# Loads moved up into the decay stage, and the sums split and turned inside the state chain

## The chip, the cores and the metric

The kernel runs on one core of a Trainium2 chip. The metric is the device time of one execution in microseconds.

## The reference

One inference step of a hybrid backbone, depth 1, for two requests that share weights: 128 context tokens and 2048 latent tokens, model width 1024. The layer adds a token mixer and then a mixture of 16 experts:

```python
h = rms_norm(x, norm_mix_g) * (1 + sc_a) + sh_a
u_pool, z, xbc, dt_raw = split(h @ w_in)
y_pool = multiscale_pool(u_pool, pool_w, pool_scale)
xs, bm, cm = split(silu(centred_depthwise_conv(xbc, conv_w, conv_b)))
dt_f, dt_b = softplus(dt_raw + dt_bias)              # 8 heads each way
y_f, h_f = ssd_chunked_scan(xs, dt_f, -exp(a_log_fwd), bm, cm, h0_fwd)
y_b, h_b = ssd_chunked_scan(reversed ..., h0_bwd)     # chunks of 128 tokens
y = rms_norm((y_f + y_b + d_skip * xs) * silu(z), ssm_norm_g)
x = x + g_a * (concat(y_pool, y) @ w_out)
h = rms_norm(x, norm_ffn_g) * (1 + sc_m) + sh_m
x = x + g_m * expert_choice_ffn(h, w_router, w_gate, w_up, w_down)
```

Inside a scan, with `a_cum` the cumulative sum of `dt * a` over the 128 tokens of a chunk:

```python
cb = cc @ bc^T ;  y_diag = (cb * exp(a_cum[l] - a_cum[s], l >= s)) @ X
chunk_state = bc^T @ (X * exp(a_cum[-1] - a_cum))
h_next = h * exp(a_cum[-1]) + chunk_state             # serial over chunks
y_off  = (cc @ h_enter) * exp(a_cum)
```

## The kernel before

The kernel is a row of stages: `front` (norm, input projection, convolution, pooling, adaLN), `decays`, `back_states`, `mixer`, `selection`, `experts`, `final`. Each stage opens a block in which every engine has its own list of instructions; the next stage's instructions start when all engines have come to the end of theirs. DMAs still in flight may cross that border. Tokens are handled in 17 tiles of 128, tile 0 being the context. `front` leaves its results in the DRAM tensor `mixed`: 16 slots of 128 channels by 2176 tokens, of which slots 0 to 3 are the pooled part, 4 to 7 z, 8 to 11 x, 12 and 13 B, 14 and 15 C.

`decays` makes, for all tiles at once, a table `tab` of dt, its product with the rate, the exponentials of the sums, the weight of each token towards its chunk's end (`T_WEND`) and each chunk's decay (`T_DEC`). ScalarE loads an activation table and takes two exponentials (of the rates, L984, and of -|v|, L986). VectorE works out a softplus by a polynomial (L1032 to L1045, each step waiting for the one before). GpSimd fills and cuts the masks and the selector `pick` (L966 to L978). TensorE spreads the gate rows (L1007) and sums over tokens with triangular matrices. At the end VectorE splits the sums `v` into three bf16 parts in `stack` (L1058 to L1062), TensorE turns the 17 tiles of `stack` (L1019) and ScalarE copies them to `acum_t` (L998, L999), which only `mixer` reads.

`back_states` runs the backward chain of states. SP loads the two initial states and then one chunk at a time (six slots of `mixed`, 384 KB) into two buffers `xb`. TensorE turns the states (L1135), makes the router's shift rows (L1140, 16 matmuls), and then in round n turns chunk n (`turn`, L1150 and L1152) and multiplies chunk n-1 (`states`, L1163). ScalarE copies the B part (`bt`, L1184) and rounds one eighth of W_out (L1192), whose 512 KB it asks for itself (L1173, L1188) as soon as one of two staging buffers is free. VectorE in round n weights chunk n (`weigh`, L1212), carries the state over chunk n-1 (`carry`: decay L1221, add L1226) and makes the low part of an eighth of W_out (`low_w`, L1203). GpSimd stores each state (256 KB, two buffers `hb`) to the DRAM tensor `back` (L1109), and ends when all stores have landed.

`mixer` then takes the 17 tiles in order: SP loads `mz` (z, x, B, C), `hbt` (the stored state), `mp` (pooled part) and `xs` (residual rows) for tile i into two buffers each, the first two tiles at once. TensorE first adds up the decay exponents of tile 0 (`decay_rows`, from `acum_t`), ScalarE takes their exponentials, and then tile 0 is turned (L1364) and copied (L1501).

## Time and profile before

| what | value |
|---|---|
| median of 3 runs | 2522.24 us (2519.3 to 2522.86) |
| profiled execution, its own time | 2521.52 us |
| its span in the profile | 2519.9 us |
| TensorE busy in the span | 90% |
| VectorE / ScalarE / GpSimd busy | 55% / 40% / 9% |

The span is the profiled execution from its first instruction to its last; its own time is measured around it. All stretches below are in microseconds from the span's start. A duration behind an instruction's name is that of the group in its line; the bracket is how long the engine sat idle before it, and what released it.

### The profile page before, as it was taken

The page shows a single profiled execution, that of the slowest core. Times are in us where ns is not written, and L with a number is a line of the kernel's source. Part 1 is how long each engine was busy: PE and PEld are TensorE (multiplying, and loading weights), DVE is VectorE, ACT ScalarE, POOL GpSimd, SP SyncE. Part 2 cuts the span into 40 slices and gives each one's busy share as a digit, 9 for nine tenths or more (in the row PEclk, how much of TensorE's full clock was granted, in tenths as well). Part 3 has the DMA queues.
Part 4 walks back from the last instruction along what each step waited for, and adds up shares of the span by engine and source line. Part 5 has one row for each costly group of instructions (what it writes and reads, how often), then busy time and mean ns, then how long its engine had stood idle before and what let it go on. Part 6 is the DMA issues. An engine that isn't in the chain of part 4 may idle for free. (4 is left out here: it accounts for less than half of the span.)

```text
span 2519.9 us, 40046 instructions
## 1 busy us (share of the span) xinstructions
PE 2261.8 (90%) x15772; PEld 2052.0 (81%) x15772; DVE 1381.2 (55%) x2184; ACT 998.2 (40%) x1734; POOL 238.3 (9%) x307
## 2 busy tenths in 40 slices
PE   4999999956799999629999999999999999999980
PEld 2878887855688887518999999999999999999980
DVE  2655443226477777464566456655565555645543
ACT  3642222222455554104444444444444344434424
POOL 0000000021111111000100111101010110011010
PEclk8999999987799999758999999999999999999995
DMA  8533442216344443033665565656565655556537
GB/s 277 180 114 120 144 144 96 88 60 223 91 138 138 139 139 117 34 118 103 192 195 167 176 193 177 200 160 187 176 209 154 183 181 188 173 176 188 176 94 285
DMA packets 318699, 396.57 MB, mean 157 GB/s; under 512 B 12014, under 2 KB 273150, under 8 KB 316558
## 3 DMA queue, kind: packets, MB, share of 16 engines
q1 hardware_dynamic: 287406, 287.67, 35.7%
q0 software_dynamic: 22400, 86.06, 11.7%
q10 hardware_dynamic: 8800, 21.56, 2.3%
q8 instruction: 62, 1.02, 0.2%
q14 instruction: 31, 0.25, 0.0%
HBM read 318.12 MB, written 77.14 MB: 157 GB/s over the span
## 5 line engine op out<-in xcount | busy, mean ns | idle before, releaser
L2227 DVE TENSOR_TENSOR experts_wlo<-experts_raw,experts_whi 128x2048 fp32r<-128x2048 f32 x192 | 439.9, 2291 | 421.8 <-ACT experts_whi L2171 421.8
L2109 PE MATMUL experts_ps_r<-experts_xhi,experts_whi 128*128 128x272 f32 x2048 | 605.2, 296 | 5.4 <-DVE experts_xlo L2281 5.4
L2109 PE MATMUL experts_ps_r<-experts_xhi,experts_wlo 128*128 128x272 f32 x2048 | 593.8, 290 | 0.0
L2109 PE MATMUL experts_ps_r<-experts_xlo,experts_whi 128*128 128x272 f32 x2048 | 590.5, 288 | 0.0
L2109 PEld LDWEIGHTS experts_ps_r<-experts_xhi,experts_whi 128*128 128x128 f32 x2048 | 386.1, 189 | 8.5 <-DVE experts_xlo L2281 5.5
L2109 PEld LDWEIGHTS experts_ps_r<-experts_xlo,experts_whi 128*128 128x128 f32 x2048 | 386.9, 189 | 0.0
L2109 PEld LDWEIGHTS experts_ps_r<-experts_xhi,experts_wlo 128*128 128x128 f32 x2048 | 386.1, 189 | 0.0
L2171 ACT ACTIVATE experts_whi<-experts_raw 128x2048 fp32r<-128x2048 f32 x192 | 366.1, 1907 | 14.6 <-DMA experts_raw<-in_w_gate 13.8
L2109 PE MATMUL experts_ps_r<-experts_hhi,experts_whi 128*128 128x272 f32 x1024 | 299.6, 293 | 0.2 <-DVE experts_hlo L2301 0.2
L2109 PE MATMUL experts_ps_r<-experts_hhi,experts_wlo 128*128 128x272 f32 x1024 | 296.3, 289 | 0.0
L2109 PE MATMUL experts_ps_r<-experts_hlo,experts_whi 128*128 128x272 f32 x1024 | 294.8, 288 | 0.0
L521 PE MATMUL front_ps<-front_hhi,front_whi 128*128 128x384 f32 (+1 forms) x640 | 236.1, 369 | 0.0
L521 PE MATMUL front_ps<-front_hhi,front_wlo 128*128 128x384 f32 (+1 forms) x640 | 230.8, 361 | 0.0
L521 PE MATMUL front_ps<-front_hlo,front_whi 128*128 128x384 f32 (+1 forms) x640 | 230.8, 361 | 0.0
L2195 ACT ACTIVATE experts_hhi<-experts_hid 128x272 fp32r<-128x272 f32 x128 | 55.2, 431 | 353.9 <-DVE experts_hid L2298 353.9
L2109 PEld LDWEIGHTS experts_ps_r<-experts_hhi,experts_whi 128*128 128x128 f32 x1024 | 192.7, 188 | 1.1 <-DVE experts_hlo L2301 0.5
L2109 PEld LDWEIGHTS experts_ps_r<-experts_hlo,experts_whi 128*128 128x128 f32 x1024 | 193.0, 188 | 0.0
L2109 PEld LDWEIGHTS experts_ps_r<-experts_hhi,experts_wlo 128*128 128x128 f32 x1024 | 192.6, 188 | 0.0
L521 PEld LDWEIGHTS front_ps<-front_hhi,front_whi 128*128 128x128 f32 x640 | 120.8, 189 | 25.4 <-ACT front_u L659 12.6
L659 ACT ACTIVATE front_u<-front_ps 128x128 f32<-128x128 f32 (+2 forms) x90 | 40.2, 469 | 248.9 <-PE front_ps L521 227.9
L2049 POOL DMA_INDIRECT x<-experts_yo,experts_idx x48 | 72.1, 1502 | 684.1 <-DVE experts_yo L2288 521.1
L2190 ACT ACTIVATE experts_sg<-experts_ps_r 128x272 f32<-128x272 f32 x128 | 51.0, 398 | 214.9 <-PE experts_ps_r L2109 214.9
(393 smaller groups left out, 3453.5 us busy)
## 6 DMA issues: line engine op xcount, KB each, us to landing
experts_raw<-in_w_gate SPq DMA_DIRECT2D x64, 1024.0 KB, 5.0
experts_raw<-in_w_up SPq DMA_DIRECT2D x64, 1024.0 KB, 5.0
experts_raw<-in_w_down SPq DMA_DIRECT2D x64, 1024.0 KB, 5.3
shared_whalf<-in_w_ada SPq DMA_DIRECT2D x16, 1024.0 KB, 5.2
mixer_mz<-mixed SPq DMA_DIRECT2D x17, 768.0 KB, 7.9
mixed<-front_acc POOLq DMA_DIRECT2D x9, 1024.0 KB, 4.2
resid<-early_xin POOLq DMA_DIRECT2D x17, 512.0 KB, 3.7
mixer_xs<-resid SPq DMA_DIRECT2D x17, 512.0 KB, 4.0
```

Of the source, the lines that this page charges most:

```text
L521: mm = pe.matmul(ps[:, out, 0:n], wt[buf][:, kk, :], h[:, kk, t0:t0 + n], start=(kk == 0 and q == 0), stop=(kk == KD - 1 and q == 2))
L659: ins = act.activation(dst_u[:, uo:uo + pn], ps[:, bank_of(s), po:po + pn], func)
L2049: pool.indirect_dma_start(io["x2"], bass.IndirectOffsetOnAxis(idx[2][0:n, a:a + 1], 0), yo[0:n, a, :], None, compute_op=ALU.add).then_inc( ...
L2109: mm = pe.matmul(dst, w[:, c % RING, kk, cols], r[:, kk, :], start=(kk == 0 and q == 0), stop=(kk == KD - 1 and q == 2))
L2171: act.activation(whi[:, c % RING, :, :], raw[:, c % RAW, :, :], ACT.Copy).then_inc(whi_done, 1)
L2190: act.activation(sg[:, ft % 2, :], ps_r[:, (2 * ft) % 4, 0:ROWS], ACT.Silu).then_inc(silu_done, 1)
L2195: act.activation(hhi[:, ft, :], hid[:, ft % 2, :], ACT.Copy).then_inc(hhi_done, 1)
L2227: dve.tensor_tensor(wlo[:, c % RING, :, :], raw[:, c % RAW, :, :], whi[:, c % RING, :, :].bitcast(F32), ALU.subtract).then_inc(wlo_done, 1)
```

## The change

In `decays`, SP now issues the loads of both states and of the first four chunks, and ScalarE issues all eight loads of W_out before its first exponential. GpSimd clears `wrs` and the zero half of `hf` there, behind the masks. The split of the sums, their turning and copying leave `decays`: VectorE does the five steps of the split in `back_states` between the decay and the add of `carry`, in rounds 1, 2 and 3 (`between`); TensorE turns four tiles of sums at a time in rounds 4 to 8 (`turn_sums`) into one PSUM bank, and ScalarE copies them in its rounds 5 to 9. The low parts of W_out come in rounds 4 to 11 and the router's weights in round 12. The shift rows are made in round 2, behind the first two products. The chunk buffer is four deep, the state buffer three deep, W_out is staged whole. The loops over rounds, which ran partly in registers, are written out. At its end SP loads the first two tiles of `mixer`, whose SP begins with the one state of tile 1.

```diff
-        v, mag, e, z, z2, poly, relu = (k.sb(f"sp_{n}", [P, NT, HH]) for n in ("v", "mag", "e", "z", "z2", "poly", "relu"))
+        v = g.v_acum
+        mag, e, z, z2, poly, relu = (k.sb(f"sp_{n}", [P, NT, HH]) for n in ("mag", "e", "z", "z2", "poly", "relu"))
         aexp = k.sb("aexp", [P, HH])
-        rest = k.sb("rest", [P, NT, HH])
-        stack = k.sb("stack", [P, NT, N3], BF16)
...
+
+        @block.sync
+        def _(sp):
+            for d, name in enumerate(("state_ssm_fwd", "state_ssm_bwd")):
+                sp.dma_start(g.st[:, d, :, :], io[name][0, 0].rearrange("(a h) d n -> (h d) a n", a=4)).then_inc(g.st_loaded, 16)
+            for n in range(NB_X):
+                load_back(sp, g, io, n)
...
+            pool.memset(g.wrs[:, :, :, :], 0.0)
+            pool.memset(g.hf[:, 0, :], 0.0)
...
             act.preload_act_table_set("natural_log_exp_and_others")
-            act.activation(aexp[:, :], g.rows[:, R_ALOG:R_ALOG + HH], ACT.Exp).then_inc(aexp_done, 1)
+            w_out = io["w_out"][0].rearrange("(k p) n -> p k n", p=P)
+            for kk in range(KD):
+                act.dma_start(g.stg[:, kk, :], w_out[:, kk, :]).then_inc(g.wo_loaded[kk // 4], 16)
+            act.activation(aexp[:, :], g.rows[:, R_ALOG:R_ALOG + HH], ACT.Exp).then_inc(scalar_done, 1)
             act.wait_ge(mag_done, 1)
-            act.activation(e[:, :, :], mag[:, :, :], ACT.Exp, scale=-1.0).then_inc(exp_done, 1)
+            act.activation(e[:, :, :], mag[:, :, :], ACT.Exp, scale=-1.0).then_inc(scalar_done, 1)
...
-            act.wait_ge(acum_turned, 1)
-            act.activation(g.acum_t[:, 0:T - P], ps_acum[0:N3, 0:T - P], ACT.Copy)
-            act.activation(g.acum_t[:, T - P:T], ps_f[0:N3, :, :].rearrange("p t h -> p (t h)")[:, 0:P], ACT.Copy)
...
-            pe.wait_ge(made, 3)
-            pe.wait_ge(row_copied, 2)
-            pe.wait_ge(stack_done, 1)
-            for i in range(NT):
-                out = ps_acum[0:N3, P * i:P * i + P] if i < NT - 1 else ps_f[0:N3, :, :].rearrange("p t h -> p (t h)")[:, 0:P]
-                mm = pe.matmul(out, stack[:, i, :], g.identb[:, :], start=True, stop=True)
-            mm.then_inc(acum_turned, 1)
...
-            link(dve.tensor_copy(stack[:, :, 0:HH], v[:, :, :]))
-            link(dve.tensor_tensor(rest[:, :, :], v[:, :, :], stack[:, :, 0:HH], ALU.subtract))
-            link(dve.tensor_copy(stack[:, :, HH:2 * HH], rest[:, :, :]))
-            link(dve.tensor_tensor(rest[:, :, :], rest[:, :, :], stack[:, :, HH:2 * HH], ALU.subtract))
-            dve.tensor_copy(stack[:, :, 2 * HH:N3], rest[:, :, :]).then_inc(stack_done, 1)
-            dve.wait_ge(exps_done, 2)
+            dve.wait_ge(scalar_done, A_DECAYS)
             dve.tensor_tensor(tab[:, :, T_WEND:T_WEND + HH], mag[:, :, :], tab[:, :, T_DT:T_DT + HH], ALU.mult)
...
+NB_X = 4
+
+
+def load_back(sp, g, io, n):
+    sp.dma_start(g.xb[:, n % NB_X, :, :], io["mixed"][8:14, :, P * (16 - n):P * (17 - n)].rearrange("s p t -> p s t")
+                 ).then_inc(g.xb_loaded[n % NB_X], 16)
+
+
+def load_tile(sp, g, io, i):
+
+    b, cols = i % 2, slice(P * i, P * i + P)
+    sp.dma_start(g.mz[:, b, :, :], io["mixed"][4:16, :, cols].rearrange("s p t -> p s t")).then_inc(g.mz_loaded[b], 16)
+    sp.dma_start(g.mp[:, b, :, :], io["mixed"][0:4, :, cols].rearrange("s p t -> p s t")).then_inc(g.mp_loaded[b], 16)
+    sp.dma_start(g.xs[:, b, :], io["resid"][cols, :]).then_inc(g.xs_loaded[b], 16)
+
...
+    NB_H = 3
     with ExitStack() as ctx:
         k = Kit(nc, ctx, "back_states")
-        st = k.sb("st", [P, 2, 4, NS])
-        xb = k.sb("xb", [P, 2, 6, P])
+        st, xb, stg = g.st, g.xb, g.stg
+        stack, rest = k.sb("stack", [P, NT, N3], BF16), k.sb("rest", [P, NT, HH])
...
+        hb = k.sb("hb", [P, NB_H, 512])
...
         def _(pool):
-            pool.wait_ge(settled, 1)
...
+            for n in range(N + 1):
+                if n == 0:
                     pool.wait_ge(st_copied, 2)
                 else:
-                    hold(pool, settled, (h_done, n))
-                pool.dma_start(io["back"][bass.ds(n, 1), :, :].rearrange("o p c -> (o p) c"), hb[:, b, :]
-                               ).then_inc(hb_stored[b], 16)
-
-            over_tiles(pool, N + 1, [(store, 0)])
-            for b in range(2):
-                pool.wait_ge(hb_stored[b], 16 * (N + 1) // 2)
+                    pool.wait_ge(h_done, n)
+                pool.dma_start(io["back"][n, :, :], hb[:, n % NB_H, :]).then_inc(hb_stored[n % NB_H], 16)
+            for b in range(NB_H):
+                pool.wait_ge(hb_stored[b], 16 * len(range(b, N + 1, NB_H)))
...
-                if not first_tiles(n, 2):
-                    hold(sp, settled, (turned, n - 1))
-                sp.dma_start(xb[:, b, :, :], mixed[8:14, :, bass.ds(n * -P + 16 * P, P)].rearrange("s p t -> p s t")
-                             ).then_inc(xb_loaded[b], 16)
-
-            over_tiles(sp, N, [(load, 0)])
+            for n in range(NB_X, N):
+                sp.wait_ge(turned, n - NB_X + 1)
+                load_back(sp, g, io, n)
+            for sem, value in g.mixed_stored:
+                sp.wait_ge(sem, value)
+            for i in range(2):
+                load_tile(sp, g, io, i)
...
-            pe.wait_ge(wr_loaded, 16)
-            for w in range(2):
-                for kk in range(KD):
-                    ins = pe.matmul(ps_c[:, w, :], g.mod[:, SH_M + kk, w:w + 1].broadcast_to([P, P]), wr[:, kk, :],
-                                    start=(kk == 0), stop=(kk == KD - 1))
-            ins.then_inc(shift_done, 1)
...
+                pe.wait_ge(g.xb_loaded[n % NB_X], 16 * (n // NB_X) + 16)
...
-            over_tiles(pe, N, [(turn, 0), (states, 1)])
+            def shifts():
+                pe.wait_ge(wr_loaded, 16)
+                for w in range(2):
+                    for kk in range(KD):
+                        ins = pe.matmul(ps_c[:, w, :], g.mod[:, SH_M + kk, w:w + 1].broadcast_to([P, P]), wr[:, kk, :],
+                                        start=(kk == 0), stop=(kk == KD - 1))
+                ins.then_inc(shift_done, 1)
+
+            def turn_sums(q):
+                pe.wait_ge(stack_chain, 5)
+                if q:
+                    pe.wait_ge(acum_copied, q)
+                tiles = range(4 * q, min(4 * q + 4, NT))
+                for i in tiles:
+                    mm = pe.matmul(ps_a[0:N3, P * (i % 4):P * (i % 4) + P], stack[:, i, :], g.identb[:, :], start=True, stop=True)
+                mm.then_inc(acum_turned, 1)
+
+            for n in range(N + 1):
+                if n < N:
+                    turn(n)
+                if n:
+                    states(n - 1)
+                if n == 2:
+                    shifts()
+                if 4 <= n < 9:
+                    turn_sums(n - 4)
...
             act.dma_start(wr[:, :, :], io["w_router"][0].rearrange("(k p) e -> p k e", p=P)).then_inc(wr_loaded, 16)
-            for kk in range(2):
-                act.dma_start(stg[:, kk, :], w_out[:, kk, :]).then_inc(wo_loaded[kk], 16)
             act.wait_ge(st_turned, 1)
+            act.activation(hb[:, 0, :], ps_s[:, 1, :], ACT.Copy).then_inc(st_copied, 1)
             act.activation(g.hf[:, 1, :], ps_s[:, 0, :], ACT.Copy).then_inc(st_copied, 1)
-            act.activation(hb[:, 0, :], ps_s[:, 1, :], ACT.Copy).then_inc(st_copied, 1)
-            act.wait_ge(shift_done, 1)
-            act.activation(g.shift_l[:, :, :], ps_c[:, :, :], ACT.Copy)
...
                 if n < KD:
-                    if n >= 2:
-                        act.wait_ge(wo_lo, n - 1)
-                        act.dma_start(stg[:, b, :], w_out[:, n, :]).then_inc(wo_loaded[b], 16)
-                if 1 <= n <= KD:
-                    kk = n - 1
-                    act.wait_ge(wo_loaded[kk % 2], 16 * (kk // 2 + 1))
-                    act.activation(g.wohi[:, kk, :], stg[:, kk % 2, :], ACT.Copy).then_inc(wo_hi, 1)
+                    act.wait_ge(g.wo_loaded[n // 4], 64)
+                    act.activation(g.wohi[:, n, :], stg[:, n, :], ACT.Copy).then_inc(wo_hi, 1)
+                if n == 3:
+                    act.wait_ge(shift_done, 1)
+                    act.activation(g.shift_l[:, :, :], ps_c[:, :, :], ACT.Copy)
+                if 5 <= n < 10:
+                    q = n - 5
+                    w = min(512, T - 512 * q)
+                    act.wait_ge(acum_turned, q + 1)
+                    act.activation(g.acum_t[0:N3, 512 * q:512 * q + w], ps_a[0:N3, 0:w], ACT.Copy).then_inc(acum_copied, 1)
...
-                if n >= 1:
-                    dve.wait_ge(hb_stored[1 - b], 16 * ((n + 1) // 2))
-                dve.tensor_tensor(hb[:, 1 - b, :], tmp[:, :], ps_s[:, b, :], ALU.add).then_inc(h_done, 1)
+                if n + 1 >= NB_H:
+                    dve.wait_ge(hb_stored[to], 16 * ((n + 1) // NB_H))
+                dve.tensor_tensor(hb[:, to, :], tmp[:, :], ps_s[:, n % 2, :], ALU.add).then_inc(h_done, 1)
+
+            def low_w(kk):
+                dve.wait_ge(wo_hi, kk + 1)
+                dve.tensor_tensor(g.wolo[:, kk, :], stg[:, kk, :], g.wohi[:, kk, :].bitcast(F32), ALU.subtract)
+
+            def sum_parts(n):
+
+                v = g.v_acum
+                at = stack[:, :, HH * (n // 2):HH * (n // 2) + HH]
+                if n:
+                    dve.wait_ge(stack_chain, n)
+                src = v if n < 2 else rest
+                if n % 2 == 0:
+                    ins = dve.tensor_copy(at, src[:, :, :])
+                else:
+                    ins = dve.tensor_tensor(rest[:, :, :], src[:, :, :], at, ALU.subtract)
+                ins.then_inc(stack_chain, 1)
+
+            def router_weights():
+                dve.wait_ge(wr_loaded, 16)
+                for w in range(2):
+                    dve.tensor_tensor(g.wrs[:, w, :, 0:NE], wr[:, :, :], g.scale_m[:, :, w:w + 1].broadcast_to([P, KD, NE]), ALU.mult)
+
+            def between(n):
+                if n < 2:
+                    sum_parts(2 * n)
+                    sum_parts(2 * n + 1)
+                elif n == 2:
+                    sum_parts(4)
+                elif n < 3 + KD:
+                    low_w(n - 3)
+                elif n == 3 + KD:
+                    router_weights()
 
             for n in range(N + 1):
                 if n < N:
                     weigh(n)
-                if n >= 1:
-                    carry(n - 1)
-                if 2 <= n < KD + 2:
-                    low_w(n - 2)
+                if n:
+                    carry(n - 1, lambda: between(n - 1))
 
...
-            for sem, value in g.mixed_stored:
-                sp.wait_ge(sem, value)
-            for i in range(NT):
+            sp.dma_start(hb[:, 1, :], io["back"][15, :, :]).then_inc(hb_loaded[1], 16)
+            for i in range(2, NT):
                 b = i % 2
-                if i >= 2:
...
-            pool.memset(g.hf[:, 0, :], 0.0).then_inc(S["zero_made"], 1)
...
-            decays(nc, g, io)
-            back_states(nc, g, io)
+            g.mz, g.mp, g.xs = kk.sb("mz", [P, 2, 12, P]), kk.sb("mp", [P, 2, 4, P]), kk.sb("xs", [P, 2, D])
+            g.mz_loaded, g.mp_loaded, g.xs_loaded = (kk.sems(n, 2) for n in ("mz_loaded", "mp_loaded", "xs_loaded"))
+            with ExitStack() as turn:
+                kt = Kit(nc, turn, "turn")
+                g.v_acum = kt.sb("v_acum", [P, NT, HH])
+                g.st, g.xb, g.stg = kt.sb("st", [P, 2, 4, NS]), kt.sb("xb", [P, NB_X, 6, P]), kt.sb("stg", [P, KD, D])
+                g.st_loaded, g.xb_loaded, g.wo_loaded = kt.sem("st_loaded"), kt.sems("xb_loaded", NB_X), kt.sems("wo_loaded", 2)
+                decays(nc, g, io)
+                back_states(nc, g, io)
             mixer(nc, g, io)
```

## Rows read from the trace of the kernel before

**Rows 1.** Engines by stretch: length, busy us (instructions), granted clock, DMA share, GB/s.
```profile
539.10:563.80 24.70, 9.69 (x55) 8.53 (x55) 17.46 (x28) 7.36 (x11) 8.95 (x9) 0.64 0.00 0
563.80:580.10 16.30, 10.00 (x48) 10.00 (x49) 0.49 (x2) 1.28 (x3) 1.08 (x2) 0.50 0.54 165
580.10:629.90 49.80, 33.64 (x144) 24.86 (x142) 38.28 (x53) 13.21 (x23) 7.58 (x14) 0.79 0.73 236
```

**Rows 2.** Timeline of the end of `decays`: start, duration, engine, line.
```profile
557.12 0.41 ACT L995 ACTIVATE decays_sp_mag<-decays_sp_mag 128x272 f32<-128x272 f32 x1
...
559.49 1.87 PE L1019 MATMUL decays_ps_row<-ssd_identb,decays_stack 128*48 128x128 bf16 x16 [3.82 <-DVE decays_stack L1062]
...
561.50 1.87 ACT L998 ACTIVATE ssd_acum_t<-decays_ps_row 48x2048 bf16<-48x2048 f32 x1 [3.68 <-PE decays_ps_f L1019]
```

**Rows 3.** Timelines of the start of `decays`: ScalarE, GpSimd, VectorE.
```profile
540.54 0.41 ACT L986 ACTIVATE decays_sp_e<-decays_sp_mag 128x272 f32<-128x272 f32 x1
...
539.71 1.79 POOL L969 MEMSET ssd_pick<- 48x2048 bf16 x1
...
542.20 6.32 POOL L977 TENSOR_SCALAR_AFFINE_SELECT ssd_pick<-ssd_pick 48x2048 bf16<-48x2048 bf16 x3
...
540.00 1.66 DVE L1034 TENSOR_SCALAR decays_sp_relu<-decays_sp_v 128x272 f32<-128x272 f32 x1
...
544.53 2.12 DVE L1040 TENSOR_TENSOR decays_sp_z<-decays_sp_z 128x272 f32<-128x272 f32 x1
...
548.71 3.30 DVE L1043 SCALAR_TENSOR_TENSOR decays_sp_poly<-decays_sp_poly,decays_sp_z 128x272 f32<-128x272 f32 x7
```

**Rows 4.** Timeline of the opening of `back_states`, up to the first weighting.
```profile
563.84 0.53 POOL L1102 MEMSET ssd_wrs<- 128x512 f32 x1 [15.32 <-SPq L1118]
...
570.10 1.97 PE L1135 MATMUL back_states_ps_s<-kept_ident,back_states_st 128*128 128x128 f32 x8 [8.63 <-DMA back_states_st<-in_state_ssm_bwd]
...
571.86 6.85 PE L1140 MATMUL back_states_ps_c<-back_states_wr,kept_mod 128*128 128x16 f32 x32
...
578.33 0.90 PEld L1150 LDWEIGHTS back_states_ps_x<-kept_ident,back_states_xb 128*128 128x128 f32 x4
...
580.10 0.69 DVE L1212 TENSOR_TENSOR back_states_xw<-back_states_ps_x,ssd_tab 128x512 f32<-128x512 f32 x1 [12.23 <-PE back_states_ps_b L1152]
...
580.93 1.40 PEld L1163 LDWEIGHTS back_states_ps_s<-back_states_xw,back_states_bt 128*128 128x128 f32 x4
```

**Rows 5.** Timeline of the rounds of `back_states`: weightings of chunks 3 and 4, ScalarE's copies.
```profile
587.95 0.68 DVE L1212 TENSOR_TENSOR back_states_xw<-back_states_ps_x,ssd_tab 128x512 f32<-128x512 f32 x1
...
589.41 0.37 ACT L1184 ACTIVATE back_states_bt<-back_states_ps_b 128x256 f32<-128x256 f32 x1
...
591.00 0.68 DVE L1212 TENSOR_TENSOR back_states_xw<-back_states_ps_x,ssd_tab 128x512 f32<-128x512 f32 x1
...
593.36 1.06 ACT L1192 ACTIVATE ssd_wohi<-back_states_stg 128x1024 fp32r<-128x1024 f32 x1 [3.58 <-DMA back_states_stg<-in_w_out]
```

**Rows 6.** ScalarE's DMA issues by line: ns min/median/max, first and last start.
```profile
L615 ACTq DMA_DIRECT2D early_wa<-in_w_ada x4: 448/2094/10167, 0.9 to 5.7; - x4
...
L1188 ACTq DMA_DIRECT2D back_states_stg<-in_w_out x6: 334/334/335, 588.1 to 607.4; - x6
```

**Rows 7.** DMA queues from 582 to 620 us (q1 SP, q10 ScalarE, q0 GpSimd): packets, MB, share.
```profile
q1 hardware_dynamic: 9045, 4.54, 43.7%
q10 hardware_dynamic: 864, 3.15, 22.4%
q0 software_dynamic: 722, 2.37, 15.8%
```

**Rows 8.** Timeline from the last sum into `mixer`.
```profile
629.18 0.69 DVE L1226 TENSOR_TENSOR back_states_hb<-back_states_tmp,back_states_ps_s 128x512 f32<-128x512 f32 x1 [0.49 <-DMA back<-back_states_hb]
...
634.75 1.28 ACT L1492 ACT_TABLE_LOAD   x1 [8.83 <-PEq L1073]
...
640.99 0.60 ACT L1501 ACTIVATE mixer_xt<-mixer_b 128x512 f32<-128x512 f32 x1 [0.34 <-PE mixer_b L1364]
```

115 lines of the change are left out of this document (42 added, 73 removed).

## The prediction

> **What bounds the kernel now.** I read the table of engines by stretch first [rows 1]. Three serial stretches stand between `front` and `mixer`: `decays` (539.1 to 563.8 us), where no engine is busy for more than 17.5 of 24.7 us and the DMA queues stand still; the opening of `back_states` (to 580.1), 16.3 us with half a microsecond of vector work; and its fifteen rounds (to 629.9) at a granted clock of 0.79. Each ends before the next begins, so a microsecond won here is one of the span; what follows only moves forward.
>
> Then the timeline of each. In `decays` the last vector result that `back_states` needs could follow the exponential that ends at 557.53, but the split sums are turned on TensorE up to 561.4 and copied by ScalarE in 1.87 us and one short copy more [rows 2]. In the opening, TensorE waits 8.63 us for the states, turns them in 1.97, spends 6.85 on the router's shifts, and only then turns chunk 0; the first weighting is at 580.10 [rows 4]. In a round with a piece of W_out either VectorE is the bound, 3.05 us from 587.95 to 591.00, or ScalarE waits for the transfer, 3.58 us before 593.36 [rows 5].
>
> **The change, part by part.**
>
> *End of decays.* Five vector operations, 17 matmuls and two copies leave. Behind the exponential at 557.53 stands one product of 0.44 us (the size of those in [rows 3]), so the work ends near 558.0, where the copies ended near 563.5 (the next stage began at 563.8, 0.3 later) [rows 1, 2]. Gain 5.5 us.
>
> *Start of decays.* ScalarE now issues eight W_out loads behind the table load and ahead of two exponentials, and VectorE waits for the second, which ended at 540.95 [rows 3]. One issue of this load takes 334 ns; of four loads of 2 MB behind each other at the kernel's start the median took 2094 ns, the longest 10167 [rows 6]. Eight of 512 KB are the bytes of two of those, so I take 0.34 to 0.55 us each: 2.7 to 4.4 us, up to 1 us of it beside the table load, and the exponential 1.7 to 4.4 us late. Not all of it counts. VectorE is held by GpSimd today: its product at 544.53 takes 2.12 us beside three selects of 2 us (from 542.20, 6.32 in all), where the seven steps from 548.71 take 0.47 us each [rows 3]. A later chain meets the end of the selects at 548.5 all the same. Walked through (0.4, a reciprocal of 1.85, three short steps, each held where a select runs), the seven steps start at 549.6 to 552.0 and not at 548.71. Cost taken 1.4 us, bounds 0.9 and 3.3.
>
> Two fills of 128x512 come to stand behind the selects. The ReLU of 540.00 ended at 541.66, just after a fill on GpSimd (539.71 + 1.79) [rows 3]: a fill holds a tensor_scalar. Did it hold every vector operation, the new ones would cost up to 2 x 0.53 = 1.1 us [rows 4]; that is inside the bounds. The Trainium skill, page SBUF — State Buffer, section Who interferes with whom, says that an operation with two inputs from SBUF is held only by a GpSimd operation that reads SBUF, one in a two-port mode by any. The trace agrees: the ReLU was held by a fill, the two-input product by a select, which reads. By that rule the fills hold one short step at most, 0.5 us.
>
> *Opening of back_states.* It starts 5.5 - 1.4 = 4.1 us earlier, at S = 559.7. The states and four chunks were asked for from 539 on. In 38 us the SP queue moved 4.54 MB in 43.7% of the engines' time (3.66 us per MB) and ScalarE's 3.15 MB in 22.4% (2.70) [rows 7]. W_out, 4.19 MB, is then 11.3 us, the states and chunks, 2.10 MB, 7.7: 19.0 us, over near 560.5. The states are first in their queue and the chunks are used one by one, so they cost nothing here; without that cover it would be the 8.63 us of now. TensorE turns the states (1.97 us) and chunk 0, whose first load overlaps their end and whose weighting comes 1.77 us after it: S + 3.4. Turns 1 and 2 and two products follow (the first product began 2.60 us after turn 0), then, moved to n = 2, the shifts, from S + 8.5 to S + 15.4 at the low clock; chunk 3 is weighted at S + 17.2. The same distance is 587.95 - 563.8 = 24.2 us now. Gain 7.0, and if the clock rises on the way the shifts alone return half, 3.5. I take 8.0, bounds 6 and 12. Four of the five splits of the sums, 0.47 us each, lie beside the shifts.
>
> *Rounds 3 to 15.* Now from 587.95 to 629.9, 41.9 us. W_out is in SBUF, so its waits leave; the subtraction stays in eight rounds, and with it VectorE's 3.05 us. But rounds 5 to 8 get a new loop: TensorE's turn_sums(n-4) waits for ScalarE's copy of the quarter before, which stands behind bt(n) and the W_out product of round n, and these behind turn(n). At the low clock that is 1.77 for the turn [rows 4], 0.37 and 1.06 [rows 5], 0.60 for a 128x512 copy [rows 8], 0.1 for a signal and 4 matmuls of 1.87/16 [rows 2], 4.3 us; at the full clock 3.3. At the clock of 0.79 I take 3.7. Sum: round 3 2.8, round 4 3.3, four of 3.7, three of 3.05, round 12 with the router's weights 3.0, two of 2.1, the last 1.4: 38.7 us. DMA work in the stage: 11 chunks 15.8 us, 16 stores (4.19 MB in the GpSimd queue, 15.8% of 38 us for 2.37 MB) 10.6, and six tile loads, which SP issues behind the last chunk, 10.5: 37 of some 57 us [rows 7]. The tile loads fall in the last ten, where stores and chunks still run, so I add 1.0. 39.7; gain 2.2, bounds -2 and 6. A third buffer for the states gives each store three rounds.
>
> *End.* The last sum starts at 629.18 and `mixer` at 634.75: the stage waits until the last store has landed [rows 8]. Beside the tile loads I give it 0.8 us more (0 to 3). In `mixer` ScalarE waited 0.34 us for the first turn [rows 8] and then goes on behind exponentials it runs anyway: the preload gives 0.3. Net -0.5.
>
> **Sum.** 5.5 - 1.4 + 8.0 + 2.2 - 0.5 = 13.8 us off the profiled execution's 2521.52: 2507.7. The median of the three runs lies 0.7 above it, so 2508.4 in its terms, -0.55%.
>
> **The rivals.**
>
> *The full clock.* TensorE, with no pause of 9 us in the opening, is granted the full clock early: shifts 3.5 us, loop 3.3, VectorE sets all rounds. Opening 12, rounds 6, with 4.1 - 0.5 that is 21.6: 2500.6. For it: 0.79 in the rounds already. Against: 0.50 through all of 563.8 to 580.1, ten busy microseconds included [rows 1].
>
> *The wait moves.* The low clock stays and the late stores queue behind the tile loads: opening 7.0, loop 4.3 and six late rounds 0.4 longer (-2), last store 3 us late (-2.7), decays 4.1: 6.4 us, 2515.8. For it: 37 of 57 us of DMA with the heaviest part last. Against: the third buffer, and 4 chunks in flight.
>
> *No measurable change*, within 0.2% (5 us), about what a measurement here can tell. The last case with ScalarE's exponential at its latest (decays 2.2) and the opening at its least (6.0): 3.5 us, 2518.7. W_out landing late would do the same: ScalarE wants its first half at 563, some 22 us after it is asked for, with 19 us of queue work.
>
> *Slower.* One mechanism: ScalarE is held by its own queue, as at the kernel's start, where one of four issues took 10.17 us [rows 6]. If issues three to eight took half of that each, the exponential would be 30 us late. GpSimd would be done by then (3.3 us won back); the rest stands: 30 - 3.3 - 5.5 - 8.0 - 2.2 + 0.5 = +11.5, 2533.7. It decides from where ScalarE is held for 5.5 + 8.0 + 2.2 - 0.5 + 3.3 = 18.5 us. Against: all of W_out needs 11.3 us of the queues, so ScalarE would have to wait for the SP queue's transfers too.
>
> **How the numbers follow.** Near 2508.4: 0.57. Full clock: 0.20. Wait moved: 0.12. No measurable change: 0.07. Slower: 0.04. The first three are faster: 0.89. The range reaches from just below the full-clock case to just beyond the moved wait, 2499 to 2517, and leaves out the last two cases and the outer edges of the others, some 0.2 in all.
>
> **What would show it.** In `decays`, ScalarE's second exponential ending between 542.7 and 545.4, the seven steps from about 550; `back_states` near 559.7, its first weighting 3.4 us and the fourth 17 us later; rounds of 3.05 us, with 3.3 to 4.3 where sums are turned; the last sum near 616.5, `mixer` near 622. It would be wrong if ScalarE's issues took over 0.6 us each, if the states landed after 559.7, if `decays` waited for SP to finish issuing, or if rounds stayed near 4 us.

## The result and the profile after

The median fell from 2522.55 us (4 runs, 2519.3 to 2523.8) to 2498.4 us (4 runs, 2493.82 to 2499.48): a ratio of 0.9903, 95% interval 0.9886 to 0.992, 24.2 us less. The direction was forecast, the size was not: 2508.4 had been predicted, and the lower end of the range, 2499, lies 0.6 us above the measured median. The first rival, the full clock with 2500.6, which had a chance of 0.20, came within 2.2 us.

The profiled execution took 2493.82 us with a span of 2492.1, 27.8 less than before. Not all of that is the change: `decays` begins at 536.37 us instead of 539.13, behind a `front` whose code is the same in both (over all profiled executions told here its end lies between 535.2 and 540.0). So everything below is measured from the start of `decays` to the table load that opens `mixer`, 95.62 us before and 70.99 after, and 0.45 more is won up to `mixer`'s first copy: 25.1 us.

| us | before | after | won | predicted |
|---|---|---|---|---|
| `decays` | 24.66 | 20.10 | 4.6 | 4.1 |
| start of `back_states` to the first weighting | 16.31 | 3.29 | | |
| start of `back_states` to the fourth weighting | 24.16 | 10.92 | 13.2 | 8.0 |
| fourth weighting to the last sum | 41.23 | 34.90 | 6.3 | 2.2 |
| last sum to `mixer` | 5.57 | 5.07 | 0.5 | -0.8 |
| `mixer` to its first copy | 6.24 | 5.79 | 0.4 | 0.3 |

The table of engines by stretch, of the kernel after. Columns: start and end, length, busy us (instructions) of PE, PEld, DVE, ACT, POOL, granted clock, DMA share, GB/s.

```profile
536.30:556.40 20.10, 7.65 (x38) 6.71 (x38) 13.63 (x23) 5.10 (x9) 9.84 (x11) 0.67 0.93 313
556.40:559.80 3.40, 3.29 (x16) 3.33 (x17) 0.04 (x1) 1.12 (x3) 0.00 (x0) 0.50 0.18 19
559.80:602.30 42.50, 31.72 (x193) 25.53 (x191) 38.45 (x60) 15.30 (x29) 8.12 (x15) 0.94 0.83 260
```

Compare it with [rows 1]. The DMA queues, which stood still in `decays`, now move 313 GB/s there; the opening shrank from 16.3 us to 3.4; and the rounds have a granted clock of 0.94 where they had 0.79. VectorE is busy there for 38.45 us (38.28 before), with the splits of the sums and the router's weights added (60 instructions, 53 before), in 42.5 us instead of 49.8: it is the bound now, busy for 90%.

The timeline of `decays` after:

```profile
536.40 4.62 ACTq L992 DMA_DIRECT2D turn_stg<-in_w_out  x8
...
541.19 0.41 ACT L995 ACTIVATE decays_sp_e<-decays_sp_mag 128x272 f32<-128x272 f32 x1
...
539.39 6.28 POOL L981 TENSOR_SCALAR_AFFINE_SELECT ssd_pick<-ssd_pick 48x2048 bf16<-48x2048 bf16 x3
...
545.73 0.52 POOL L984 MEMSET ssd_wrs<- 128x512 f32 x1
...
546.08 0.44 DVE L1037 TENSOR_TENSOR decays_sp_z<-decays_sp_z 128x272 f32<-128x272 f32 x1
...
546.90 3.30 DVE L1040 SCALAR_TENSOR_TENSOR decays_sp_poly<-decays_sp_poly,decays_sp_z 128x272 f32<-128x272 f32 x7
...
555.76 0.44 DVE L1055 TENSOR_TENSOR ssd_tab<-decays_sp_mag,ssd_tab 128x272 f32<-128x272 f32 x1 [0.47 <-ACT decays_sp_mag L1004]
```

ScalarE issues for 4.62 us and its exponential is 3.4 us late (it ends 5.23 us into the stage, 1.82 before), but the seven steps start only 0.95 later (10.53 us in, 9.58 before): they come after GpSimd's selects either way. The stage ends with the one product, no turning and no copy behind it [rows 2].

The opening, where the products' time tells the clock:

```profile
556.50 1.94 PE L1127 MATMUL back_states_ps_s<-kept_ident,turn_st 128*128 128x128 f32 x8 [2.65 <-PEq L943]
...
559.76 0.69 DVE L1211 TENSOR_TENSOR back_states_xw<-back_states_ps_x,ssd_tab 128x512 f32<-128x512 f32 x1 [3.56 <-PE back_states_ps_b L1138]
...
563.00 3.64 PE L1158 MATMUL back_states_ps_c<-back_states_wr,kept_mod 128*128 128x16 f32 x32
...
567.39 0.69 DVE L1211 TENSOR_TENSOR back_states_xw<-back_states_ps_x,ssd_tab 128x512 f32<-128x512 f32 x1 [1.26 <-PE back_states_ps_b L1138]
```

The 8.63 us of waiting for the states is gone, and the shifts, 6.85 us in [rows 4], take 3.64. (The shifts are 16 matmuls in the program and 32 records in the profile.) The table by windows shows the clock there, and how it fell again behind the shifts:

```profile
560.00:563.00 3.00, 3.00 (x20) 2.74 (x19) 2.62 (x6) 2.98 (x6) 0.42 (x1) 0.94 0.51 148
563.00:567.00 4.00, 4.00 (x38) 4.00 (x37) 3.09 (x6) 0.66 (x1) 1.09 (x2) 1.00 1.03 315
567.00:571.00 4.00, 4.00 (x17) 3.42 (x15) 2.94 (x6) 2.04 (x5) 0.54 (x1) 0.57 0.56 164
```

A middle round of VectorE, and the end of the stage:

```profile
576.25 0.68 DVE L1211 TENSOR_TENSOR back_states_xw<-back_states_ps_x,ssd_tab 128x512 f32<-128x512 f32 x1
576.85 0.68 DVE L1220 TENSOR_TENSOR back_states_tmp<-back_states_hb,ssd_tab 128x512 f32<-128x512 f32 x1
577.45 1.22 DVE L1230 TENSOR_TENSOR ssd_wolo<-turn_stg,ssd_wohi 128x1024 fp32r<-128x1024 f32 x1
578.59 0.68 DVE L1226 TENSOR_TENSOR back_states_hb<-back_states_tmp,back_states_ps_s 128x512 f32<-128x512 f32 x1
579.18 0.68 DVE L1211 TENSOR_TENSOR back_states_xw<-back_states_ps_x,ssd_tab 128x512 f32<-128x512 f32 x1
...
602.29 0.69 DVE L1226 TENSOR_TENSOR back_states_hb<-back_states_tmp,back_states_ps_s 128x512 f32<-128x512 f32 x1 [0.58 <-DMA back<-back_states_hb]
603.28 0.54 POOL L1108 DMA_DIRECT2D back<-back_states_hb  x1 [1.45 <-DVE back_states_hb L1226]
...
607.36 1.28 ACT L1512 ACT_TABLE_LOAD   x1 [10.57 <-PEq L1078]
```

VectorE's four operations of a round follow each other without idle time (none is marked), and the next weighting comes 2.93 us after the one before: eight of the fourteen distances are 2.93 or 2.94. In [rows 5] ScalarE waited 3.58 us for W_out in such a round. TensorE and ScalarE are not as fast as VectorE in the rounds in which sums are turned: three turns of the sums wait 1.12 us each for ScalarE's copy of the quarter before, and the first four start 3.20, 3.17 and 3.17 us apart:

```profile
574.53 0.38 PE L1168 MATMUL back_states_ps_a<-ssd_identb,back_states_stack 128*48 128x128 bf16 x4 [1.12 <-ACT ssd_acum_t L1202]
...
577.70 0.38 PE L1168 MATMUL back_states_ps_a<-ssd_identb,back_states_stack 128*48 128x128 bf16 x4 [1.12 <-ACT ssd_acum_t L1202]
```

VectorE does not feel it, because each chunk is turned ahead of its weighting. That lead shrinks by 0.24 us a round, from 0.78 us to 0.06, and these rounds are over before it is gone. At the end the last sum waits 0.58 us for a store, and the stage ends when its own store has landed.

### The profile page after: what moved, and what is told of

Same layout as the page of the kernel before. It is cut to its first block and busy times, and to the rows that moved or that the text cites. A ratio compares the mean times of both kernels' runs of the same rounds, so it can differ in the third digit from the quotient of the medians.

```text
span 2492.1 us, 39889 instructions
## 1 busy us (share of the span) xinstructions
PE 2249.2 (90%) x15772; PEld 2042.8 (82%) x15772; DVE 1377.6 (55%) x2184; ACT 996.9 (40%) x1737; POOL 238.3 (10%) x307
```

## The experiments

My theory for the 11 us that I had not foreseen, called the clock theory in the expectations: TensorE has no long pause in the opening any more, so the full clock is granted early (in the kernel after it rises 3.9 us into `back_states`, at 560.37), which halves the shifts and the turns and leaves VectorE as the only bound of the rounds. The rivals: the gain is in the transfers alone (states, chunks, W_out at hand, whatever the clock), or in the depth of the buffers, which I had costed at nothing. All times below are of one execution each unless said otherwise. "Stretch" is from the start of `decays` to the start of `mixer`. The kernels ran on three chips, on which the kernel before took 2521.14 us, 2515.48, and 2514.27 (median of 7, 2511.27 to 2520.95), so stretches and stages are compared, not whole times. Whole times also scatter behind the stretch: from `mixer`'s first copy to the end the profiled executions take 1873.9 to 1883.5 us, and one of them (the shifts first again) 1890.4, though the kernels do the same there.

### The kernel before once more

> The kernel before, unchanged, profiled once more, to see how far its stages vary. If the rounds of 41.2 us are its own, they come out within 1 us and the states' stage needs 65.4 us from its start to the last sum again. If they depend on when the clock rises, as the 38 us in the two variants of it suggest, they come out 1 to 4 us shorter with the opening unchanged at 24.2.

No edit. 2517.79 us; stretch 96.21 (95.62), `decays` 24.66 (24.66), fourth weighting 25.29 us into `back_states` (24.16), from there to the last sum 40.68 (41.23). In this one repetition a stage came within 1.1 us, the stretch within 0.6 and `decays` within 0.01; a difference of a stage below 1.1 us is not told apart from this.

### States and two chunks asked for early, nothing else

```diff
--- before
+        @block.sync
+        def _(sp):
+            for d, name in enumerate(("state_ssm_fwd", "state_ssm_bwd")):
+                sp.dma_start(g.st[:, d, :, :], ...).then_inc(g.st_loaded, 16)
+            for n in range(2):
+                sp.dma_start(g.xb[:, n, :, :], ...).then_inc(g.xb_loaded[n], 16)
```

> The kernel before, with only the loads of the two states and of the first two chunks issued in the decay stage. Loads alone (my prediction's view, clock low through the opening): the 8.63 us wait goes, states 1.97, shifts 6.85 and turns stay at the low clock, chunk 3 is weighted about 18 us after the stage starts and not 24.2. Clock theory: without the pause TensorE is granted the full clock some 5 us into the stage, the shifts halve, chunk 3 is weighted 13 to 15 us after the start. In both the rounds stay near 41 us.

2514.97 us, stretch 86.88: 8.7 less than before. The first weighting comes 10.68 us into the stage, the fourth 18.51. The shifts stay at the low clock:

```profile
564.67 7.01 PE L1146 MATMUL back_states_ps_c<-back_states_wr,kept_mod 128*128 128x16 f32 x32 [0.30 <-DMA back_states_wr<-in_w_router]
```

So the early loads alone win 5.65 us up to the fourth weighting, not 13.2; 3.1 more lie in the rounds, 38.14 us for 41.23. The clock theory as it stood fails here: the pause is gone, and the full clock did not come some 5 us into the stage but 14.0 us into it (at 576.36), behind the shifts. A missing pause is not enough.

### TensorE kept busy while it waits, no early load

28 turns of the identity, whose results nothing reads, ahead of the wait for the states.

```diff
--- before
+            for i in range(28):
+                pe.transpose(ps_x[:, 0, P * (i % 4):P * (i % 4) + P], g.ident[:, :], g.ident[:, :])
             pe.wait_ge(st_loaded, 32)
```

> The kernel before, with 28 turns of the identity (results unused) on TensorE while it waits for the states; no load is moved. Clock theory: the full clock is granted before the states land, so states 1.0 and shifts 3.5 us, and chunk 3 is weighted 4 to 6 us earlier than 24.2 us after the stage starts. If the low clock of the opening has another cause, or does not matter, the distance stays 24 us or grows.

2516.39 us, stretch 87.53: 8.1 us won with no load moved in the program. PE's timeline:

```profile
562.15 5.56 PE L1133 MATMUL back_states_ps_x<-kept_ident 128*128 128x128 f32 x28 [2.36 <-PEq L943]
...
568.41 1.09 PE L1137 MATMUL back_states_ps_s<-kept_ident,back_states_st 128*128 128x128 f32 x8 [0.71 <-DMA back_states_st<-in_state_ssm_bwd]
...
569.35 3.64 PE L1142 MATMUL back_states_ps_c<-back_states_wr,kept_mod 128*128 128x16 f32 x32
```

The states' turns take 1.09 us instead of 1.97 and the shifts 3.64 instead of 6.85 [rows 4]; the fourth weighting is at 19.47, and the rounds behind it are 3.4 us shorter as well. In the opening this is the clock by itself, and no theory of transfers alone gives it. For the rounds it is less certain. In the four executions whose code there is that of the kernel before, the way from the fourth weighting to the last sum and the mean granted clock on it are 41.23 us and 0.79 (before), 40.68 and 0.87 (before once more), 38.14 and 0.91 (early loads), 37.84 and 0.95 (this one). The two go together, but fewer waits could also be what raised the clock, and no run lowers the clock in the rounds alone.

### The shifts first again, in the kernel after

```diff
--- after
+            shifts()
             for n in range(N + 1):
...
-                if n == 2:
-                    shifts()
```

> The changed kernel with the router's shifts ahead of chunk 0 again. Clock theory: the shifts start about 3 us in, when their weights land, partly at the low clock, 4.5 to 5.5 us; chunk 3 is weighted 14 to 16 us after the stage starts (changed kernel 10.9). Low clock throughout: 19 us. If the place of the shifts did not matter: 11 us.

2512.29 us, stretch 76.50, 5.5 longer. (The whole time is up by more, because `experts`, with the same code, took 9.5 us longer in this execution.) The first weighting is 7.5 us later (10.76), the fourth 6.6 (17.53). The window of TensorE around them:

```profile
560.40:567.00 6.60, 6.60 (x31) 6.60 (x32) 0.00 (x0) 0.72 (x2) 0.55 (x1) 0.50 0.10 40
```

TensorE is never idle in it and the granted clock stays 0.50; the expectation that they would run partly at the full clock and take 4.5 to 5.5 us failed, they took 7.01. Between the first and the fourth weighting lie 6.77 us here without the shifts and 7.63 after with them: where the change puts them they cost 0.9 us, beside VectorE's work.

### W_out in the rounds again, each piece asked for one round ahead

```diff
--- after
-            for kk in range(KD):
-                act.dma_start(g.stg[:, kk, :], w_out[:, kk, :]).then_inc(g.wo_loaded[kk // 4], 16)
...
+                    if 1 <= n < KD - 1:
+                        act.dma_start(stg[:, n + 1, :], w_out[:, n + 1, :]).then_inc(g.wo_loaded[(n + 1) % 2], 16)
+                    act.wait_ge(g.wo_loaded[n % 2], 16 * (n // 2) + 16)
```

> The changed kernel with W_out asked for by ScalarE in the rounds again, each eighth one round ahead, into its own buffer. If W_out's early load matters by itself: a transfer of 4 to 6 us asked for one round ahead makes the eight rounds 4 to 5 us, and the way from chunk 3 to the last sum 40 to 45 us (changed kernel 34.9), while the decay stage gets 1 us shorter since ScalarE's exponential is on time. If the clock alone made the rounds short, they stay at 2.93 us and the way at 35.

2502.77 us, stretch 76.43, 5.4 longer. `decays` is 0.96 shorter (19.14: the exponential is back at its old place) and the opening the same (11.04), but the rounds take 41.18 us, with distances of 7.50, 4.09 and 3.60 among those of 2.94. The waits say why: ScalarE waited 10.4 us for W_out in 7 waits, the longest 4.8.

### The sums split, turned and copied in `decays` again

```diff
--- after
+            act.wait_ge(acum_turned, 1)
+            act.activation(g.acum_t[:, 0:T - P], ps_acum[0:N3, 0:T - P], ACT.Copy)
...
+            for i in range(NT):
+                mm = pe.matmul(out, stack[:, i, :], g.identb[:, :], start=True, stop=True)
...
-                if 4 <= n < 9:
-                    turn_sums(n - 4)
```

> The changed kernel with the split, the turns and the copies of the sums back at the end of the decay stage. My terms: that stage 5.5 us longer (25.6 us), the opening as in the changed kernel (10.9), the rounds 34.9 less 0.25 us in each of four and 0.45 in one, 33.5; in all 4 us slower. If the moved sums were what loaded the rounds (my loop of 3.7 us), the rounds would fall by 3 us and the two would nearly cancel.

2505.01 us, stretch 76.04. `decays` takes 25.61, 5.51 more, behind the long copy:

```profile
562.22 1.87 ACT L1011 ACTIVATE ssd_acum_t<-decays_ps_row 48x2048 bf16<-48x2048 f32 x1 [3.69 <-PE decays_ps_f L1031]
```

`back_states` is 0.4 shorter up to the last sum (45.38 for 45.82). The move is worth 5.1 us.

### `mixer`'s tiles loaded in `mixer` again

`load_tile(0)` and `load_tile(1)` go from the end of `back_states`' SP list to the head of `mixer`'s.

```diff
--- after
-            for i in range(2):
-                load_tile(sp, g, io, i)
...
+            load_tile(sp, g, io, 0)
             sp.dma_start(hb[:, 1, :], io["back"][15, :, :]).then_inc(hb_loaded[1], 16)
+            load_tile(sp, g, io, 1)
```

> The changed kernel with the first two tiles of the mixer loaded by the mixer again. My term: the mixer's first copy 0.3 to 0.45 us later (6.2 and not 5.8 us after its start). If the tile loads crowd the last stores: the two waits of 1.6 us on stores in the last rounds go, rounds 33.5 and not 34.9, so that the preload costs more than it gives. If not, 34.9 stays.

2496.68 us. `mixer`'s first copy comes 7.73 us into it instead of 5.79, behind a wait for the tile:

```profile
612.29 1.11 PE L1386 MATMUL mixer_b<-kept_ident,ssd_mz 128*128 128x128 f32 x4 [1.86 <-DMA ssd_mz<-mixed]
```

The stretch is 1.4 us shorter (69.62), though: the last two sums no longer wait for stores and come 1.92 and 1.45 us behind the one before, instead of 2.94 and 1.99. The preload wins 1.9 us in `mixer` and gives 1.4 back through the stores that its transfers run beside. The 0.6 left is less than what a stage repeats to, so whether the preload gains anything in all is not shown. My term of 0.3 to 0.45 us for it in `mixer` was too small.

### TensorE kept busy in `decays` too

64 turns of the identity ahead of the sums, 20 behind them.

```diff
--- after
+            for i in range(64):
+                pe.transpose(spare, g.ident[:, :], g.ident[:, :])
             pe.wait_ge(da_done, 1)
...
+            for i in range(20):
+                pe.transpose(ps_row[:, 0, 0:P], g.ident[:, :], g.ident[:, :])
```

> The changed kernel with 64 and 20 turns of the identity (results unused) on TensorE in the decay stage, where it waits. Clock theory: the full clock is there when the states' stage opens, the states take 1.0 and not 1.94 us, chunk 0 is weighted 2.0 and not 3.3 us after the start and chunk 3 at 8.8 to 9.5 and not 10.9; the rest as before. If the clock is not what the opening depends on: 10.9. It could cost up to 0.5 us in the decay stage where the sums wait behind the last turns.

2496.02 us, stretch 68.85, 2.1 less. The clock is full from 560.08 on, 0.5 us ahead of the stage. The rows show the end of `decays` and the start of the stage:

```profile
556.31 4.01 PE L1023 MATMUL decays_ps_row<-kept_ident 128*128 128x128 f32 x20
...
560.63 1.07 PE L1133 MATMUL back_states_ps_s<-kept_ident,turn_st 128*128 128x128 f32 x8 [0.30 <-PEq L943]
...
565.65 3.64 PE L1164 MATMUL back_states_ps_c<-back_states_wr,kept_mod 128*128 128x16 f32 x32
```

The first weighting is at 1.79 instead of 3.29, and the stage is 2.65 shorter to the last sum. `decays` is 0.51 longer, but not because the sums wait for the turns ahead of them: they start 15.31 us into it in both kernels. It is longer because the twenty turns behind them take 4.01 us, most of it at a granted clock of 0.50 (556.67 to 560.08), and end later than VectorE's last product did.

### The exponentials ahead of the loads of W_out

The loop of eight issues goes behind ScalarE's two exponentials.

```diff
--- after
-            for kk in range(KD):
-                act.dma_start(g.stg[:, kk, :], w_out[:, kk, :]).then_inc(g.wo_loaded[kk // 4], 16)
             act.activation(aexp[:, :], g.rows[:, R_ALOG:R_ALOG + HH], ACT.Exp).then_inc(scalar_done, 1)
...
             act.activation(e[:, :, :], mag[:, :, :], ACT.Exp, scale=-1.0).then_inc(scalar_done, 1)
+            for kk in range(KD):
+                act.dma_start(g.stg[:, kk, :], w_out[:, kk, :]).then_inc(g.wo_loaded[kk // 4], 16)
```

> The changed kernel with ScalarE's two exponentials ahead of the W_out loads. My account of the decay stage: the exponential ends 1.8 us after the stage starts and not 5.2, but GpSimd's selects hold VectorE, so the seven steps start 0.95 us earlier (9.6 and not 10.5) and the stage is 19.1 and not 20.1 us. If GpSimd did not hold it, the steps would start 3.4 us earlier. W_out's first half lands 2 us later, without effect.

2494.04 us, stretch 69.17, 1.8 shorter; only the half of it that lies in `decays` is this edit's. The rest, 0.9 us in a stage with the same code, is within what a stage repeats to; in this execution the clock stayed at 1.00 behind the shifts. The exponential ends 1.83 us in, the seven steps start at 9.57 (9.58 before, 10.53 after), `decays` takes 19.15. So the issues cost 0.95 us, and what held VectorE before them is GpSimd:

```profile
540.78 2.12 DVE L1037 TENSOR_TENSOR decays_sp_z<-decays_sp_z 128x272 f32<-128x272 f32 x1
```

### Chunks and states two deep

```diff
--- after
-NB_X = 4
+NB_X = 2
...
-    NB_H = 3
+    NB_H = 2
```

> The changed kernel with the chunk and the state buffers two deep as before (two chunks asked for in the decay stage). If the depth carries the rounds: a chunk asked for when the one two before it is turned lands 4 to 5 us later, against a round of 2.9 twice, so single rounds wait 1 us, and the last short rounds wait for stores, 2 to 5 us more than 45.4 from the stage's start to the last sum. If the depth is not used: within 1 us of it.

2503.14 us, stretch 81.11: 10.1 longer, the most of any part undone, where 2 to 5 had been expected. `decays` and the first weighting are as after (20.09, 3.30); chunk 3 comes 6.23 us behind chunk 2 instead of 3.97, the four rounds in which sums are turned take 3.17 to 3.23, the next ones 2.93 to 2.97, and the last distance is 5.83. The 3.17 us are the loop through ScalarE that the kernel after hides: here the chunks come too late for TensorE to gain a lead, and VectorE waits for it. TensorE waited 7.3 us for chunks in 7 waits, VectorE 7.1 us for stores in 2, of which the longer:

```profile
606.02 0.69 DVE L1226 TENSOR_TENSOR back_states_hb<-back_states_tmp,back_states_ps_s 128x512 f32<-128x512 f32 x1 [3.94 <-DMA back<-back_states_hb]
```

Of the 10.1 us, 3.5 lie ahead of the fourth weighting, 1.1 in the rounds and 5.5 in the last sums, where VectorE waits for stores. The 3.5 are not the wait alone: TensorE waited 1.6 us for chunk 2, and the clock then fell to 0.50 during the shifts (4.16 us) and stayed there to 575.28. What each depth costs by itself was not run.

### The shifts first, and TensorE busy in `decays`

The edits of two kernels above together.

> The changed kernel with the router's shifts ahead of chunk 0 (17.5 us to chunk 3, the shifts 7.0 us at the low clock) and turns of the identity on TensorE in the decay stage. If the place of the shifts matters by the clock: they run at the full clock in 3.6 us behind a wait of 1 us for their weights, and chunk 3 is weighted 11.5 to 13 us after the start. If 16-column products lose the clock whatever came before: 7.0 us again, 16 to 17.5.

2501.7 us, stretch 77.86. The expectation that the shifts run at the full clock failed. Windows of the pause and of the shifts, and PE's timeline:

```profile
557.00:559.00 2.00, 0.00 (x0) 0.00 (x0) 0.00 (x0) 1.03 (x2) 0.55 (x1) 0.94 0.31 30
558.80:559.15 0.35, 0.00 (x0) 0.00 (x0) 0.00 (x0) 0.00 (x0) 0.09 (x1) 0.50 0.00 0
559.20:566.00 6.80, 6.80 (x32) 6.80 (x33) 0.00 (x0) 0.00 (x0) 0.00 (x0) 0.50 0.10 39
```

```profile
559.17 7.01 PE L1164 MATMUL back_states_ps_c<-back_states_wr,kept_mod 128*128 128x16 f32 x32 [2.25 <-DMA back_states_wr<-in_w_router]
```

The clock was 0.94 in the 2 us before, in which TensorE waited for the router's weights. It fell to 0.50 inside that pause, at 558.77, 0.4 us ahead of the first shift, so the shifts did not bring it down; but they ran for 7 us without bringing it back. In the seven kernels in which they took 3.64 us (after, the busy wait, W_out in the rounds, the sums in `decays`, no tile loads, the busy `decays`, the exponentials first) they followed other products with no idle time marked ahead of them, and more of these than the eight turns of the states that precede them in [rows 4].

### What the experiments point to

Exponentials ahead of the loads; two of GpSimd's selects behind `da_done` and the third in `back_states`; 44 and 16 turns of the identity in `decays`; the shifts behind the last round.

```diff
--- after
+            pool.wait_ge(da_done, 1)
+            for n in range(2):
+                cut_pick(pool, g, n)
...
+            for i in range(44):
+                pe.transpose(spare, g.ident[:, :], g.ident[:, :])
...
-                if n == 2:
-                    shifts()
                 if 4 <= n < 9:
                     turn_sums(n - 4)
+            shifts()
```

> The changed kernel and four steps that the runs point to: exponentials ahead of the W_out loads; two of GpSimd's selects behind the softplus and one in the states' stage; TensorE kept busy in the decay stage by 44 and 16 turns of the identity; the router's shifts behind the last round, beside the last store. My account: decay stage 20.1 - 0.95 - 3.3 = 15.9 us, stage start to last sum 45.4 - 2.0 - 1.8 = 41.6, tail 5.1: 62.6 us to the mixer (changed kernel 71.0), near 2490 us. If the selects hold VectorE at their new place too, the decay stage is 17 to 18 us; if the shifts lengthen the tail, it is 6 us or more.

2486.6 us (median of 4, 2485.76 to 2490.51) against 2514.27: ratio 0.9884, interval 0.9866 to 0.9903. That interval overlaps the one of the change, so the ratios alone don't part the two; the stretch does, 65.02 against 70.99. Rows of its `decays` and after:

```profile
544.70 0.44 DVE L1043 TENSOR_TENSOR decays_sp_z<-decays_sp_z 128x272 f32<-128x272 f32 x1
...
545.51 3.30 DVE L1046 SCALAR_TENSOR_TENSOR decays_sp_poly<-decays_sp_poly,decays_sp_z 128x272 f32<-128x272 f32 x7
...
553.38 1.69 DVE L1061 TENSOR_TENSOR ssd_tab<-decays_sp_mag,ssd_tab 128x272 f32<-128x272 f32 x1 [0.47 <-ACT decays_sp_mag L1004]
...
558.75 1.11 PE L1149 MATMUL back_states_ps_x<-kept_ident,turn_xb 128*128 128x128 f32 x4 [0.72 <-DMA turn_xb<-mixed]
...
597.20 3.98 PE L1171 MATMUL back_states_ps_c<-back_states_wr,kept_mod 128*128 128x16 f32 x32
```

The product that took 2.12 us beside a select takes 0.44 with the selects gone, and the seven steps start 6.18 us into the stage. A select that runs late holds one product for 1.69 us instead. The shifts, at the end, take 3.98 us beside the last store and cost nothing. The way to the last sum fell short of the expectation, 43.98 us for 41.6, and all of that is in the opening. `decays` is now 16.0 us long, less than the 19 us of its transfers; chunk 1 lands late, and TensorE waits 0.72 us for it. The clock is a second reason:

```profile
556.00:562.70 6.70, 5.98 (x25) 5.11 (x24) 3.02 (x6) 3.74 (x6) 1.95 (x2) 0.50 0.97 244
```

The sixteen turns end 2.15 us before TensorE's next work, the clock fell to 0.50 at 555.96, 0.6 us into the stage, and the first weighting came 2.74 us into the stage, where the busy `decays` had 1.79. How much each of the two costs was not run by itself.

## Why the prediction was right or wrong

S is the start of `back_states`, as in the prediction.

**End of decays, +5.5: right.** Undone by itself it costs 5.51 us there, and 0.4 comes back in the rounds.

**Start of decays, -1.4: right mechanism, 0.95 measured**, just above the lower bound of 0.9. ScalarE's eight issues took 4.62 us (378 to 999 ns, median 496), where 2.7 to 4.4 had been taken, and the exponential was 3.4 us late, inside 1.7 to 4.4. GpSimd's selects hid the rest, as argued: with the exponential back in its place the steps start at 9.57, with the selects moved at 6.18. The rule of the Trainium skill (page SBUF — State Buffer, section Who interferes with whom) that a product with two inputs from SBUF is held by a reading GpSimd operation and not by a fill agrees with these traces: such a product takes 0.44 us beside a fill (546.08 in the kernel after), and 1.69 to 2.12 beside a select. The slower rival, ScalarE held by its own queue, did not occur.

**Loads, 19.0 us of work: right.** The share of 0.93 over 20.1 us is 18.7 us of work for 6.29 MB. The last of the four chunks landed at 556.88, just behind the start of `back_states`, and nothing there waited for a load. SP's issues did take up to 6.64 us each, and held nothing that `decays` waits for.

**Opening, +8.0: the failed step.** It was costed "S + 8.5 to S + 15.4 at the low clock" for the shifts, with a turn of 1.77 us behind them; only 1.0 of the 8.0 us was for a clock that might rise. The first weighting came at S + 3.3 as said (S + 3.4). Then the clock rose: the shifts ran from S + 6.5 for 3.64 us, the fourth weighting was at S + 10.9 instead of S + 17.2, and the gain 13.2, beyond the bound of 12. What I had taken as the evidence against, "0.50 through all of 563.8 to 580.1, ten busy microseconds included", was read too widely: most of those ten are the shifts, and what they do to the clock says little of turns and state products. In the four kernels with them ahead of the chunks and no extra turns directly before them (before, the early loads alone, the shifts first, the shifts first behind a busy `decays`) they ran at 0.50 throughout; with chunks' turns and products ahead they began at the full clock and, but for the two-deep kernel, kept it to their end. My own rival had named the wrong reason, too: taking the pause away does not raise the clock by itself, as the early loads alone show; the shifts had to move. Keeping TensorE busy with turns alone in the kernel before gave the full clock and 8.1 us.

**Rounds 3 to 15, +2.2: the same error.** "At the clock of 0.79 I take 3.7" for the four rounds with a turn of the sums: they took 2.93, which is 3.1 of the 4.8 us by which the rounds beat the forecast. The granted clock was 1.00 in these rounds, and the loop through ScalarE, 3.3 by my sum at that clock, took 3.17. That alone would give about two thirds of the 3.1; the rest is that TensorE entered these rounds with a lead, so that VectorE never waited for the loop, which the sum had left out. The three plain rounds, 3.05 forecast, are 2.93. The round of the router's weights, 3.0 forecast, is 2.20. Gain 6.3, bound 6. It all rests on W_out being at hand: asked for in the rounds again it costs 6.3 us there, the whole gain.

**Depth of the buffers: costed at nothing, 10.1 us when undone.** The walk through the rounds assumed no wait for chunks and 1.0 us for the tile loads beside the stores, so the total did not suffer by it; but what makes that true is the depth. At two deep the faster rounds run into both transfers.

**End, -0.5: wrong sign, small.** The last store was not 0.8 later; the tail is 0.5 shorter, 0.4 of it because GpSimd issues the store 0.99 us after the sum begins, and not 1.39. The tile loads do collide, but earlier, in the last rounds' store waits: 1.05 and 0.58 us, which are gone in the kernel without the preload. In `mixer` the preload gives 0.45 against before, and 1.9 against leaving it out of the changed kernel.

**All together.** The parts undone one by one cost 5.5 (place of the shifts), 5.4 (W_out), 5.1 (sums), 10.1 (depth) and 0.6 us (tiles), 26.7 in all for 25.1 won. They are not independent, and the early load of the states, 8.7 us alone in the kernel before, is not among them. For the opening the cause, the clock, is shown from both sides: raised without moving a load, and lowered by moving the shifts alone. For the rounds it is in part argued: the loop's time at the full clock is measured, but no run holds the clock down there and leaves all else. Why the shifts do not raise the clock stays open; only their shape and place were seen.

## What to carry to other kernels

Ask of each low-clock stretch what TensorE did in it, not only whether it was busy. Here it paid to put turns and larger products first and the narrow ones behind them or at the end. Work out what a removed pause is worth at both clocks. Where an early load shortens a stage, walk the rounds again at the faster pace before calling a buffer's depth free. Where two loops run at different paces (3.17 and 2.93 us here), ask how long the faster one can live on its lead. Before sparing a wait on one engine, look which engine releases the next step: 3.4 us on ScalarE cost 0.95 here, and 3.4 more lay under GpSimd's selects.

## What the runs showed of the hardware

- The 32 product records of 128x16 ran for 6.85 to 7.01 us without a pause at a granted clock of 0.50, in four kernels; in one of them it had been 1.00 until 0.4 us ahead of them, in a pause of 2.25 us. Where it was up as they began and TensorE had not paused, they took 3.64 us (seven kernels).
- In the 4 us that followed them the clock was 0.57 to 0.62 in five of these seven kernels (0.57 in the kernel after), and 1.00 in two (the busy `decays`, the exponentials first). The exponentials first has the same `back_states` as the kernel after, so what decides this is not shown.
- One of SP's fifteen issues for chunks took 6.64 us while the loads of W_out were under way (median 0.36); ScalarE's eight issues for 4.19 MB took at most 1.0 us each.
- Six tile loads behind the last chunk cost the stores of the same rounds 1.4 us, in one pair of runs.
